# One inference step with windowed attention and PEER retrieval: attention as one sequence of 32 heads, softmax shares on ScalarE, 64 candidate key sums instead of 256

## The chip, the cores and the metric

One NeuronCore of one Trainium2 chip runs the whole program. The metric is the time of one execution on the device in microseconds (us), as a median of several. The engines are TensorE (PE, its weight loads PEld), VectorE (DVE), ScalarE (ACT), GpSimd (POOL) and SyncE (SP). Each works through its own list of instructions in order, and semaphores tie the lists together.

## The reference

Two layers, for 128 prompt tokens (one tile of 128, group P) and 512 latent tokens (four tiles, group S). Each layer computes, per token group:

```python
h = x * (1 + scale1) + shift1
q, k, v, su, sv = split(h @ w_in)              # 8 query heads, 2 kv heads of 64; su, sv of 512 go through gelu
attn = softmax([sink, q k^T / 8 + mask]) @ v   # P: its own block; S: neighbour blocks + 128 cached keys, rotary q, k
sg   = su * (w_s @ layer_norm(sv) + b_s)       # 8 groups, 128x128 position mixing
x  = layer_norm(ALPHA * x + gate1 * (concat(attn, sg) @ w_o)) * g1 + b1
h2 = x * (1 + scale2) + shift2
# PEER: per token and each of 8 heads
s1, s2 = (q half 1) @ key1.T, (q half 2) @ key2.T        # 128 scores each
t1, i1 = top_k(s1, 16);  t2, i2 = top_k(s2, 16)
top, pos = top_k(t1[:, None] + t2[None, :], 16)          # of 256 sums
idx = i1 * 128 + i2 at pos;  g = softmax(top)
y = sum over 8 x 16 experts of gelu(u_tab[idx] . h2) * g * v_tab[idx]
x  = layer_norm(ALPHA * x + gate2 * y) * g2 + b2
```

Since t1 and t2 are sorted, the sum of place i of t1 and place j of t2 (from 0) has at least (i+1)(j+1)-1 sums that are no smaller; the best 16 sums therefore lie among the pairs with (i+1)(j+1) <= 16.

The modulation vectors of both layers (24 pieces of 512 columns from w_mod, 2 MB each) are computed once, spread over the first group P of layer 0. Outputs are both x and the prompt's k and v.

## The kernel before

**Stages of a layer.** Group P runs through projection, attention, output projection, norm, PEER queries and key scores; then group S does the same with four tiles. Then come a dense PEER stage over all 128 blocks of the U table (PE, loop over b, tiles 3 and 4), the building of one-hot matrices and gates (DVE and PE), and the dense V stage (128 blocks, tiles 3, 4, 1). Tiles 0, 1 and 2 take their U rows by gather instead (POOL, line 548, 128 rows of 4 KB per partition, so 512 KB a gather, ring of 8 slots), and DVE multiplies each gathered row set with h2 and sums (`dot_rows`, line 1079); tiles 0 and 2 do the same with V rows (`add_rows`, line 1097).

**What sets the order.** There is no planner. `plan_jobs` (line 140) lists which PSUM bank each product takes and in which order; each engine's code is written out in an order that fits, and waits are counted per bank (`full`, `emptied`). SP's list holds the weight slots (ring of 8 slots of 512 KB, `w_ring`), and the row broadcasts: before the first `query` slot it waits for the last `yT` and then loads five rows into `row5`, lines 413 to 421. PE follows the same order (`attend`, line 652), ACT likewise (line 845), DVE likewise (line 1301 and the loop at line 1354).

**Attention before (per tile).** PE transposes the queries (line 649), makes three heads' scores (line 662), then the spatial gate (line 686); per head it makes one more head's scores, waits for the shares, transposes them (line 696), and weighs the values in two halves (line 672) after heads 5 and 7. DVE takes a head's scores out of PSUM with mask and maximum (line 1318) and, two heads later, adds the sink, takes the reciprocal and multiplies the exponentials (lines 1309 to 1311). ACT makes the exponentials (lines 855, 857) and copies transposed shares out of PSUM (line 863). In group S the DVE puts two `dot_rows` of tile 0 after each head. All four `norm_sv` (line 1293) come ahead of the first tile's attention, 32 of the 128 rows go into `take_qk` (line 1276), 16 come ahead of the norms and 16 between them.

**Choosing (per tile).** `half_keys` (line 1103) takes the best 16 of 128 scores, 16 times. `best_pairs` (line 1123) writes 4 heads x 256 sums and takes the best 16 of each head with five instructions over 256 columns; it runs twice. `split_positions` (line 1142) turns a place of the 256 into a pair. `pick` (line 1151) looks up the indices. ACT takes the softmax's exponential in `top_softmax` (line 883); for tile 0 it stands at the end of group P on ACT, ahead of group S's first copies at line 895. Tile 0 is chosen at the end of P, tile 1 at the end of S, tiles 3 and 4 in the dense U stage (ACT has `top_softmax(3)` after block 44), tile 2 in the dense V stage.

## Time and profile before

| | us |
|---|---|
| median of 3 runs (4259.37 to 4267.57) | 4263.49 |
| the profiled execution, its own time | 4257.01 |
| its span, first to last instruction | 4255.2 |
| PE busy, mean granted clock 0.914 | 3651.7 |
| DVE busy | 3039.6 |
| POOL busy | 1679.7 |
| ACT busy | 552.8 |
| moved by DMA | 1263.24 MB, 297 GB/s on average |

Read it so: a large busy share of PE or DVE does not say that the engine bounds a stage; which wait ends last in a stage does. "PEclk" is the clock granted to TensorE: 1.00 is 2.4 GHz, 0.50 is 1.2 GHz, and numbers between are a mix of the two within the stretch. A DMA share near 1 means that all 16 DMA engines are occupied.

### The profile page before, as it was taken

How to read it: one execution, taken by the hardware profiler on the slowest of the kernel's cores; microseconds unless marked ns; L12 is line 12 of the kernel's file. 1: busy time of each engine (PE TensorE's matmuls, PEld its weight loads, DVE VectorE, ACT ScalarE, POOL GpSimd, SP SyncE). 2: the span in 40 equal slices, each digit the busy share in tenths (PEclk: the TensorE clock that was granted, in tenths of full speed). 3: DMA queues.
4: the chain of work that ended last, by engine and by line, in shares of the span. 5: the costliest groups of instructions: out<-in, count | busy, mean ns of one | idle time of the engine just before them, and what ended most of it. 6: DMA issues, size and time to landing. Idle time of an engine off the chain costs nothing.

```text
span 4255.2 us, 38282 instructions
## 1 busy us (share of the span) xinstructions
PE 3651.7 (86%) x12502; PEld 2179.4 (51%) x12502; DVE 3039.6 (71%) x6640; ACT 552.8 (13%) x1349; POOL 1679.7 (39%) x1410
## 2 busy tenths in 40 slices
PE   8889478999997689898986846899999868989897
PEld 2334244588896434343435424458888743434333
DVE  0348865889957897656665888578996689766567
ACT  0101230111122200000001013011112220000000
POOL 3225640524312146556510465052341214555453
PEclk9899679999998999999988866999999899999998
DMA  9667762989986679999964676388998758999995
GB/s 319 234 206 300 257 218 93 341 312 349 341 318 253 242 285 381 395 397 393 395 244 160 251 268 213 117 307 300 350 370 303 273 208 319 351 393 397 397 391 233
DMA packets 458901, 1263.24 MB, mean 297 GB/s; under 512 B 40448, under 2 KB 143616, under 8 KB 452560
## 3 DMA queue, kind: packets, MB, share of 16 engines
q0 software_dynamic: 198912, 721.61, 45.3%
q1 hardware_dynamic: 234384, 455.22, 30.2%
q10 hardware_dynamic: 25408, 83.96, 4.9%
q8 instruction: 101, 1.65, 0.2%
q14 instruction: 96, 0.79, 0.1%
HBM read 1173.81 MB, written 86.84 MB: 296 GB/s over the span
## 4 chain that ended last, share of the span: by engine, by line
PE 41%; DVE 33%; DMA 19%; issue 3%; POOL 3%; ACT 1%; SPq 0%; DVEq 0%; ACTq 0%
DMA w_ring<-in_peer_v_dram 11%; PE P L811 10%; DVE ring L1079 8%; PE P L784 7%; PE P L760 6%; DMA ring<-in_peer_u_dram,eidx 5%; PE T L811 4%; DVE late L1097 3%; PE P L626 3%; DVE h L1229 3%; POOL ring L548 3%; DVE h L1225 2%; PE O L584 2%; DMA h<-acts_d 2%; PE V L584 2%
## 5 line engine op out<-in xcount | busy, mean ns | idle before, releaser
L548 POOL DMA_INDIRECT ring<-in_peer_u_dram,eidx x768 | 940.0, 1224 | 1398.8 <-DVE ring L1079 857.0
L811 PE MATMUL P<-w_ring,area 128*128 128x512 f32 x2048 | 959.8, 613 | 136.0 <-DMA w_ring<-in_peer_v_dram 74.1
L548 POOL DMA_INDIRECT ring<-in_peer_v_dram,eidx x512 | 656.4, 1282 | 916.9 <-DVE late L1097 453.4
L1079 DVE SCALAR_TENSOR_TENSOR ring<-ring,h 128x1024 f32<-128x1024 f32 x768 | 918.3, 1222 | 115.0 <-DMA ring<-in_peer_u_dram,eidx 106.1
L784 PE MATMUL P<-hT,w_ring 128*128 128x256 f32 x4096 | 900.8, 380 | 16.9 <-ACT late L954 16.7
L784 PEld LDWEIGHTS P<-hT,w_ring 128*128 128x128 f32 x4096 | 775.5, 191 | 121.6 <-ACT late L954 18.0
L811 PEld LDWEIGHTS P<-w_ring,area 128*128 128x128 f32 x2048 | 401.3, 197 | 655.3 <-issue 571.4
L811 PE MATMUL T<-w_ring,hT 128*128 128x512 f32 x1024 | 480.2, 592 | 0.0
L1097 DVE SCALAR_TENSOR_TENSOR h<-ring,dots,h 128x1024 f32<-128x1024 f32 x254 | 325.8, 1282 | 33.0 <-DMA ring<-in_peer_v_dram,eidx 17.3
L1097 DVE SCALAR_TENSOR_TENSOR late<-ring,dots,late 128x1024 f32<-128x1024 f32 x254 | 325.8, 1283 | 18.6 <-DVE late L1097 0.5
L811 PEld LDWEIGHTS T<-w_ring,hT 128*128 128x128 f32 x1024 | 194.6, 190 | 245.8 <-issue 245.8
L794 PE MATMUL T<-h 128*128 128x128 f32 x1536 | 229.2, 297 | 89.5 <-DVE h L1229 89.3
L760 PE MATMUL P<-hT,w_ring 128*128 128x128 f32 (+1 forms) x1024 | 287.3, 442 | 3.0 <-issue 2.2
L794 PEld LDWEIGHTS T<-h 128*128 128x128 f32 x1536 | 207.6, 206 | 115.0 <-issue 111.8
L1225 DVE TENSOR_TENSOR h<-qT,cst 128x512 f32<-128x512 f32 x192 | 131.7, 686 | 148.4 <-PE T L794 85.9
L760 PEld LDWEIGHTS P<-hT,w_ring 128*128 128x128 f32 x1024 | 158.4, 196 | 127.0 <-issue 122.7
L1229 DVE TENSOR_SCALAR h<-cst,qT 128x128 f32<-128x128 f32 x768 | 212.7, 339 | 0.0
L1239 DVE TENSOR_TENSOR area<-h,hT 128x256 f32<-128x256 f32 x128 | 54.3, 424 | 211.6 <-DMA h<-acts_d 175.8
L954 ACT ACTIVATE late<-P 128x256 f32<-128x256 f32 x256 | 97.9, 383 | 767.8 <-PE P L784 423.4
L696 PE MATMUL T<-ident,probs 128*128 128x128 f32 x120 | 34.9, 428 | 137.1 <-DVE probs L1311 137.1
L1239 DVE TENSOR_TENSOR area<-h,area 128x256 f32<-128x256 f32 x128 | 54.4, 425 | 123.9 <-DMA h<-acts_d 70.3
L626 PE MATMUL P<-w_ring,hT 128*128 128x512 f32 x320 | 141.5, 602 | 1.5 <-issue 1.5
(190 smaller groups left out, 2952.4 us busy)
## 6 DMA issues: line engine op xcount, KB each, us to landing
w_ring<-in_peer_uT_dram SPq DMA_DIRECT2D x256, 512.0 KB
w_ring<-in_peer_v_dram SPq DMA_DIRECT2D x256, 512.0 KB
ring<-in_w_mod_dram POOLq DMA_DIRECT2D x96, 512.0 KB, 5.9
gate_d<-area ACTq DMA_DIRECT2D x48, 1024.0 KB
w_ring<-in_peer_wq_dram SPq DMA_DIRECT2D x64, 512.0 KB
acts_d<-late ACTq DMA_DIRECT2D x128, 256.0 KB
h<-acts_d SPq DMA_DIRECT2D x64, 512.0 KB
w_ring<-in_w_in_dram SPq DMA_DIRECT2D x48, 512.0 KB
```

The source lines that it names most:

```text
L548: pool.indirect_dma_start(out=ring[:, b, :], out_offset=None, in_=tables["uv".index(phase)], in_offset=bass.IndirectOffsetOnAxis(ap=eidx[: ...
L584: mm = pe.matmul(out[0:2, :], cT[:, c, :], m_slots[:, u % MR, c % 2, :], start=c == 0, stop=c == DC - 1)
L626: mm = pe.matmul(out[:, :], hT[:, c, t * P:(t + 1) * P], w_ring[:, ws[4 * n + q], c % 2, :], start=c == 0, stop=c == DC - 1)
L760: mm = pe.matmul(out[:, 0:nt * P], w[:, c % 2, j * P:(j + 1) * P], hT[:, c, 0:nt * P], start=c == 0, stop=c == DC - 1)
L784: mm = pe.matmul(out[:, 0:TOKENS], w[:, c * P:(c + 1) * P], hT[:, c, TOKENS:2 * TOKENS], start=c == 0, stop=c == DC - 1)
L794: mm = pe.matmul(out[:, j * P:(j + 1) * P], oh_b[:, n % 2, j, :], oh_a[:, n % 2, j, :], start=True, stop=True)
L811: mm = pe.matmul(bank[ACC[2 * t + half]][:, :], w, uv_ring[:, held[b], half * 512:(half + 1) * 512], start=b == 0, stop=b == KEYS - 1)
L1079: dve.scalar_tensor_tensor(ring[:, b, :], ring[:, b, :], 1.0, h2[:, k, :], ALU.mult, ALU.mult, accum_out=dots[:, k, row:row + 1]).then_inc ...
L1097: dve.scalar_tensor_tensor(acc[k], ring[:, b, :], dots[:, k, row:row + 1], acc[k], ALU.mult, ALU.add).then_inc(row_used[b], 1)
L1225: dve.tensor_tensor(oh_b[:, n % 2], slotT[:, 1, ts].unsqueeze(2).to_broadcast([P, QUAD, KEYS]), iota128.unsqueeze(1).to_broadcast([P, QUAD ...
L1229: ins = dve.tensor_scalar(oh_a[:, n % 2, j, :], iota128, slotT[:, 0, t:t + 1], slotT[:, 2, t:t + 1], ALU.is_equal, ALU.mult)
L1239: dve.tensor_tensor(wexp_T[:, b % 4, :].rearrange("p (s t) -> p s t", t=SUB), act_in[:, b // 4 % 2, b % 4, :].rearrange("p (s t) -> p s t" ...
```

## The change

1. Group S's four tiles of eight heads run as one sequence of 32 on PE, ACT and DVE. Scores stay three heads ahead across tile borders. On PE the gate comes after head 2, the next tile's query transposes after head 4, the first half of the weighing and the transposed gate after head 6, and the second half after head 1 of the next tile.
2. The multiplication of a head's exponentials by its share moves from DVE to ACT (`den_ready`), one head behind; DVE's share of a head is taken one head late, not two.
3. `norm_sv` runs inside the sequence, after head 0 of each tile. The `dot_rows` are laid otherwise: 16 rows with the keys and values (none with the queries), 24 ahead of attention, 72 in it, and 16 behind it, ahead of the residuals.
4. ACT's `top_softmax(0)` moves behind group S's eight copies at line 895.
5. Prompt key scores go to a place of their own for all 16 half heads, so ACT waits for no free slot of `key_ring` there.
6. `best_pairs` builds 64 sums a head (1x16, 3x8, 4x4, 8x1) for all eight heads at once, four instructions, and its five instructions a head run over 64 columns. `split_positions` finds the pair with 12 instructions over all heads.
7. SP loads three of group P's five rows (gate1, ln1 gain and bias) into free parts of `area` ahead of the `w_o` slots, after a wait for the modulation rows; in S the three come where they did. The two others count on a semaphore of their own, awaited before their first use.

Fragments in this order: tiles, SP, PE, ACT (attention, `top_softmax`, prompt keys), DVE (sums, positions, attention, rows). Of attention on the three engines, `best_pairs` and `split_positions` only the new side is shown; the old side stands in the functions above.

```diff
-row5 = area[:, 0:5120].rearrange("p (r n) -> p r n", r=5)
+row5 = {g: [area[:, i * D:(i + 1) * D] for i in places]
+for g, places in (("P", (1, 3, 5, 0, 2)), ("S", (0, 1, 2, 3, 4)))}
...
+prompt_keys = area[:, 4096:6144].rearrange("p (j n) -> p j n", j=2 * PH)
...
     for kind, n, w, c0, width in plan:
+        first_rows = ((GATE1, mod_rows[l, gi, 0]), (LN1G, ln1_g[l]), (LN1B, ln1_b[l]))
+        if kind == "out" and n == 0 and g == "P":
+            for j in range(2):
+                sp.wait_ge(mod_stored[l][j], 16 * 4)
+            for r, src in first_rows:
+                sp.dma_start(row5[g][r], src.partition_broadcast(P)).then_inc(rows_in, 16)
         if kind == "query" and n == 0:
             sp.wait_ge(full[BANK["yT", g, last]], full_at(("yT", g, last), l))
-            if g == "P":
-                for j in range(2):
-                    sp.wait_ge(mod_stored[l][j], 16 * 4)
-            for r, src in ((GATE1, mod_rows[l, gi, 0]), (LN1G, ln1_g[l]), (LN1B, ln1_b[l]),
-                           (SCALE2, mod_rows[l, gi, 2]), (SHIFT2, mod_rows[l, gi, 1])):
-                sp.dma_start(row5[:, r, :], src.partition_broadcast(P)).then_inc(rows_in, 16)
+            if g == "S":
+                for r, src in first_rows:
+                    sp.dma_start(row5[g][r], src.partition_broadcast(P)).then_inc(rows_in, 16)
+            for r, src in ((SCALE2, mod_rows[l, gi, 2]), (SHIFT2, mod_rows[l, gi, 1])):
+                sp.dma_start(row5[g][r], src.partition_broadcast(P)).then_inc(late_rows_in, 16)
         for q in range(4):
...
+    nt = len(GROUPS[g])
+    heads = [(t, h) for t in range(nt) for h in range(HEADS)]
+    queries(g, 0)
+    for t, h in heads[:AHEAD]:
+        score(g, t, h)
+    for n, (t, h) in enumerate(heads):
+        if n + AHEAD < len(heads):
+            score(g, *heads[n + AHEAD])
         job = ("pT", g, t, h)
         out = begin(job)
+        pe.wait_ge(share_ready, l * (TILES * HEADS) + (GROUPS[g][t] * HEADS + h + 1))
+        for i in range(len(blocks(t)) if g == "S" else 1):
             mm = pe.transpose(out[:, i * P:(i + 1) * P], exps[h % 4][:, i * P:(i + 1) * P], ident[:])
         finish(mm, job)
+        if h == 1 and t:
+            weigh(g, t - 1, 1)
+        if h == 2:
+            gate(g, t)
+        if h == 4 and t + 1 < nt:
+            queries(g, t + 1)
         if h == 6:
+            weigh(g, t, 0)
+            gated_T(g, t)
+    weigh(g, nt - 1, 1)
...
+        if 0 < n <= len(heads):
+            t, h = heads[n - 1]
+            lo_col, hi_col = mask_cols(g, t)
+            act.wait_ge(den_ready, l * (TILES * HEADS) + (GROUPS[g][t] * HEADS + h + 1))
+            act.activation(exps[h % 4][:, 0:hi_col - lo_col], exps[h % 4][:, 0:hi_col - lo_col], ACT.Copy,
+                           scale=den[:, h:h + 1]).then_inc(share_ready, 1)
+        if n > 1:
+            t, h = heads[n - 2]
+            lo_col, hi_col = mask_cols(g, t)
+            job = ("pT", g, t, h)
+            act.activation(pT[:, h // 4, 0:(hi_col - lo_col) // P, h % 4 * P:(h % 4 + 1) * P],
+                           ready(job)[:, 0:hi_col - lo_col].rearrange("p (i n) -> p i n", n=P), ACT.Copy
                            ).then_inc(emptied[BANK[job]], 1)
+            if h == 2 and t:
+                summed_T(t - 1)
+            if h == 4 and t + 1 < nt:
+                queries(g, t + 1)
+            if h == 7:
+                job = ("yT", g, t)
+                act.activation(hT[:, 4:8, t * P:(t + 1) * P],
+                               ready(job)[:, :].rearrange("p (c n) -> p c n", c=4), ACT.Copy
+                               ).then_inc(emptied[BANK[job]], 1)
+    summed_T(nt - 1)
...
         act.activation(hT[:, c, 0:nt * P], ready(job)[:, 0:nt * P], ACT.Identity,
                        scale=mcol[:, l, 8 + c, gi:gi + 1],
                        bias=mcol[:, l, c, gi:gi + 1]).then_inc(emptied[BANK[job]], 1)
+    if g == "S":
+        top_softmax(0)
     for n, dst in ((2, su), (3, sv)):
...
                                ACT.Copy)
-            if j > 8:
-                act.wait_ge(key_used, l * (4 * PH) + (gi * 2 * PH + j - 8))
-            act.activation(key_ring[:, (j - 1) % 8, :], src[:, 0:P], ACT.Copy
-                           ).then_inc(emptied[BANK[job]], 1)
+                if j > 8:
+                    act.wait_ge(key_used, l * (2 * PH) + (j - 8))
+            act.activation(key_ring[:, (j - 1) % 8, :] if g == "S" else prompt_keys[:, j - 1, :], src[:, 0:P],
+                           ACT.Copy).then_inc(emptied[BANK[job]], 1)
             if j % 4 == 0:
                 modulation(("query", j // 4 - 1))
     modulation("end")
-    if g == "P":
-        top_softmax(0)
...
 def best_pairs(half):
+    pair = best[:].rearrange("p (h a) j -> p h a j", a=2)
+    a, b = pair[:, :, 0, :], pair[:, :, 1, :]
+    if half == 0:
+        note(dve.tensor_tensor(cand[:, :, 0:16], a[:, :, 0:1].to_broadcast([P, PH, 16]), b, ALU.add))
+        for at, i, n in ((16, 1, 3), (40, 4, 4)):
+            m = 8 if i == 1 else 4
...
+def split_positions():
+    note(dve.tensor_copy(ixf[:], best_ix[:]))
+    note(dve.tensor_single_scalar(part, pos[:], 3, ALU.logical_shift_right))
+    link(dve.tensor_single_scalar(quart, pos[:], 2, ALU.logical_shift_right))
+    link(dve.tensor_scalar(hi[:], part, 1.0, 0.0, ALU.subtract, ALU.max))
+    link(dve.scalar_tensor_tensor(hi[:], quart, -6.0, hi[:], ALU.add, ALU.max))
+    link(dve.scalar_tensor_tensor(hi[:], pos[:], -48.0, hi[:], ALU.add, ALU.max))
+    note(dve.tensor_scalar(first, hi[:], 8.0, 8.0, ALU.mult, ALU.add))
+    link(dve.tensor_scalar(lo[:], hi[:], 4.0, 24.0, ALU.mult, ALU.add))
+    link(dve.scalar_tensor_tensor(first, hi[:], 16.0, first, ALU.mult, ALU.min))
+    link(dve.tensor_tensor(first, first, lo[:], ALU.min))
+    link(dve.scalar_tensor_tensor(first, hi[:], 48.0, first, ALU.add, ALU.min))
+    link(dve.tensor_tensor(lo[:], pos[:], first, ALU.subtract))
...
+            empty(dve.tensor_tensor_reduce(exps[h % 4][:, 0:hi_col - lo_col], out[:, 0:hi_col - lo_col],
+                                           mask[:, lo_col:hi_col],
                                            HD ** -0.5, sink[:, h:h + 1], ALU.add, ALU.max,
                                            maxs[:, k % 2, h:h + 1]), job)
             dve.tensor_scalar(negmax[:, k % 2, h:h + 1], maxs[:, k % 2, h:h + 1], -1.0, None,
                               ALU.mult).then_inc(probs_max, 1)
+        if n:
+            shares(*heads[n - 1])
+        if n < len(heads):
+            if h == 0:
+                norm_sv(g, t)
+            if h == 5:
+                job = ("gate", g, t)
+                out = ready(job)
+                link(dve.tensor_tensor(tmp[:].rearrange("p (s d) -> p s d", d=HD),
+                                       out[:, :].rearrange("p (s d) -> p s d", d=HD),
+                                       bsT[:].unsqueeze(2).to_broadcast([P, SGG, HD]), ALU.add))
+                empty(dve.tensor_tensor(su[:, t, :], su[:, t, :], tmp[:], ALU.mult), job)
+            if g == "S":
+                prompt_rows(2 if h == 3 else 1)
...
+    dve.wait_ge(late_rows_in, (2 * l + (list(GROUPS).index(g) + 1)) * 32)
...
     for n in range(2):
         for t in range(nt):
             take_qk(g, n, t)
-            if latent:
+            if latent and n:
                 prompt_rows(2)
+    if latent:
+        prompt_rows(12)
     modulation("projected")
     dve.wait_ge(layer_in, (l + 1) * (16 * 8))
+    attend(g)
+    dve.wait_ge(rows_in, (2 * l + (gi + 1)) * 48)
     if latent:
         prompt_rows(8)
-    for t in range(nt):
-        norm_sv(g, t)
-        if latent:
-            prompt_rows(2)
-    for t in range(nt):
-        attend(g, t)
-    dve.wait_ge(rows_in, (2 * l + (gi + 1)) * 80)
     for t in range(nt):
         for n in range(2):
             residual(g, n, t)
...
```

## Rows read from the trace of the kernel before

**Rows 1.** Busy time by stretch: us, then PE, PEld, DVE, ACT, POOL, PEclk, DMA share, GB/s.
```profile
470.00:630.00 160.00, 104.22 (x354) 63.66 (x355) 126.25 (x330) 52.90 (x138) 87.48 (x67) 0.67 0.67 223
...
832.00:1316.00 484.00, 473.27 (x2309) 418.83 (x2308) 380.52 (x968) 77.46 (x172) 144.32 (x127) 0.99 0.89 328
...
1455.00:2188.00 733.00, 679.70 (x1536) 297.08 (x1535) 523.68 (x836) 41.52 (x128) 397.66 (x312) 0.96 0.99 371
```

**Rows 2.** Timeline where group S begins, layer 0: start us, us, instruction, [idle before <-releaser].
```profile
300.89 1.23 DVE L1126 TENSOR_TENSOR probs<-best 128x1024 f32<-128x1024 f32 x1
...
324.83 3.56 PE L721 MATMUL T<-ident,x 128*128 128x128 f32 x16 [23.77 <-ACT hT L895]
...
341.44 0.23 DVE L1176 TENSOR_SCALAR eidx<-tmp 128x128 uint32<-128x128 f32 x1
...
353.70 0.69 DVE L1267 TENSOR_TENSOR area<-T,cst 128x512 f32<-128x512 f32 x1 [12.03 <-issue]
```

**Rows 3.** Groups of DVE instructions by form, whole span: count | busy us, mean ns | idle before.
```profile
L1113 DVE MAX8 best<-left 128x8 f32<-128x128 f32 x160 | 47.1, 295 | 5.5
...
L1131 DVE MAX8 top<-probs 128x8 f32<-128x256 f32 x80 | 34.2, 428 | 2.7
```

**Rows 4.** Timeline of DVE at group S's residuals, layer 0.
```profile
640.61 0.69 DVE L1341 TENSOR_TENSOR tmp<-P,area 128x512 f32<-128x512 f32 x1 [15.33 <-DMA area<-mod_rows]
...
656.04 0.69 DVE L1341 TENSOR_TENSOR tmp<-P,area 128x512 f32<-128x512 f32 x1
...
658.63 0.69 DVE L1341 TENSOR_TENSOR tmp<-P,area 128x512 f32<-128x512 f32 x1 [1.18 <-PE P L626]
```

**Rows 5.** DVE by stretch, group S of layer 0: us, DVE busy, PEclk, DMA share, GB/s.
```profile
353.70:406.10 52.40, 51.16 (x101) 1.00 1.02 395
406.10:431.10 25.00, 19.37 (x33) 1.00 1.03 405
431.10:470.10 39.00, 36.91 (x93) 0.53 0.75 258
```

**Rows 6.** Chain of the end, pieces at layer 0: start us, us, what.
```profile
139.69 3.65 PE V L686 x16
...
446.11 4.67 DVE ring L1079 x8
```

**Rows 7.** Timeline of DVE through one head of tile 2.
```profile
528.60 0.74 DVE L1318 CUSTOM_DVE_ANT_0 probs<-P,mask,sink 128x512 f32<-128x512 f32 x1
...
529.86 0.49 DVE L1311 TENSOR_SCALAR work<-work,den 128x512 f32<-128x512 f32 x1
530.26 1.22 DVE L1079 SCALAR_TENSOR_TENSOR ring<-ring,h 128x1024 f32<-128x1024 f32 x1
...
532.55 0.74 DVE L1318 CUSTOM_DVE_ANT_0 work<-P,mask,sink 128x512 f32<-128x512 f32 x1
```

**Rows 8.** Waits from 300 to 702 us: who <- whom: us, times, longest.
```profile
DVE probs L1318 <- PE P L662: 25.1, 3, 9.5
```

**Rows 9.** Timeline of PE in the same stretch.
```profile
527.56 2.07 PE L662 MATMUL P<-kT,qT 64*128 64x384 f32 x4
530.49 1.09 PE L696 MATMUL T<-ident,work 128*128 128x128 f32 x4 [0.86 <-DVE work L1311]
...
539.27 5.40 PE L672 MATMUL O<-h,v_sb 128*128 128x512 f32 x8
```

**Rows 10.** Groups of ACT instructions by form, one tile (508 to 551 us).
```profile
L857 ACT ACTIVATE probs<-probs,negmax 128x512 f32<-128x512 f32 x4 | 2.8, 706 | 0.0
```

**Rows 11.** Timeline in the dense U stage, layer 0, ACT and PE.
```profile
1007.96 0.31 ACT L885 ACTIVATE gsm<-gsm 128x128 f32<-128x128 f32 x1 [9.46 <-DVE gsm L1139]
...
1010.02 2.50 PE L784 MATMUL P<-hT,w_ring 128*128 128x256 f32 x5 [8.91 <-ACT late L954]
```

**Rows 12.** Waits from 1525 to 1600 us, in the dense V stage.
```profile
PE P L811 <- DVE area L1239: 15.8, 4, 9.0
```

**Rows 13.** Busy time by stretch there, columns as in rows 1.
```profile
1540.00:1560.00 20.00, 9.79 (x23) 4.12 (x22) 18.86 (x54) 0.62 (x2) 2.87 (x2) 0.83 0.56 192
```

More of the change, by code:

```diff
@@ L305, in build @@
         part = left[:].bitcast(U32).rearrange("p (h j) -> p h j", h=PH)
+        first = left[:].rearrange("p (h j) -> p h j", h=PH)
         hi = sb("hi", [P, PH, TOPK])
         lo = sb("lo", [P, PH, TOPK])
+        quart = lo[:].bitcast(U32)
         r1 = sb("r1", [P, PH, TOPK])
@@ new lines, in score @@
+                def score(g, t, h):
+                    job = ("score", g, t, h)
+                    if h == 0:
+                        taken(("qT", g, t))
+                    out = begin(job)
+                    a = HD * (h // 4)
+                    for i, kb, n in runs(blocks(t) if g == "S" else [0]):
+                        mm = pe.matmul(out[:, i * P:(i + n) * P], qT[a:a + HD, h % 4, :],
+                                       kT[a:a + HD, kb:kb + n, :].rearrange("p t n -> p (t n)"), start=True, stop=True)
+                    finish(mm, job)
@@ new lines, in weigh @@
+                def weigh(g, t, kv):
+                    keyb = blocks(t) if g == "S" else [0]
+                    out = begin(("attn", g, t)) if kv == 0 else bank[BANK["attn", g, t]]
+                    taken(("pT", g, t, 4 * kv + 2))
+                    taken(("pT", g, t, 4 * kv + 3))
+                    for i, kb in enumerate(keyb):
+                        mm = pe.matmul(out[:, :], v_pad[:, kb, HD * kv:HD * kv + P], pT[:, kv, i, :],
+                                       start=kv == 0 and i == 0, stop=kv == 1 and i == len(keyb) - 1)
+                    if kv == 1:
+                        finish(mm, ("attn", g, t))
@@ L688, in attend, with gated_T @@
                     finish(mm, job)
-                    for h in range(HEADS):
-                        if h + AHEAD < HEADS:
-                            score(h + AHEAD)
+                def gated_T(g, t):
+                    taken(("gate", g, t))
+                    job = ("yT", g, t)
+                    out = begin(job)
+                    for c in range(4):
+                        mm = pe.transpose(out[:, c * P:(c + 1) * P], su[:, t, c * P:(c + 1) * P], ident[:])
+                    finish(mm, job)
@@ L692, in attend @@
+                def attend(g):
+                    nt = len(GROUPS[g])
+                    heads = [(t, h) for t in range(nt) for h in range(HEADS)]
+                    queries(g, 0)
+                    for t, h in heads[:AHEAD]:
+                        score(g, t, h)
+                    for n, (t, h) in enumerate(heads):
+                        if n + AHEAD < len(heads):
+                            score(g, *heads[n + AHEAD])
                         job = ("pT", g, t, h)
                         out = begin(job)
-                        pe.wait_ge(share_ready, l * (TILES * HEADS) + (k * HEADS + h + 1))
@@ L909, in _ @@
                     modulation("projected")
-                    for t in range(nt):
-                        attend(g, t)
+                    attend(g)
                     modulation("summed")
@@ L1011, in link, with note @@
                     dve.wait_ge(vchain, chain[0])
+                def note(ins):
+                    chain[0] += 1
+                    ins.then_inc(vchain, 1)
                 def ready(job):
@@ L1137, in softmax_in @@
+                    for h in range(4 * half, 4 * half + 4):
+                        link(dve.max(top[:, h, 0:8], cand[:, h, :]))
+                        link(dve.max_index(pos[:, h, 0:8], top[:, h, 0:8], cand[:, h, :]))
+                        link(dve.match_replace(cand[:, h, :], top[:, h, 0:8], cand[:, h, :], LOWEST))
+                        link(dve.max(top[:, h, 8:16], cand[:, h, :]))
+                        link(dve.max_index(pos[:, h, 8:16], top[:, h, 8:16], cand[:, h, :]))
                 def softmax_in(k):
@@ L1299, in norm_sv, with attend, shares @@
                     dve.wait_ge(sv_ready, l * TILES + (GROUPS[g][t] + 1))
-                def attend(g, t):
-                    k = GROUPS[g][t]
-                    lo_col, hi_col = mask_cols(g, t)
-                    width = hi_col - lo_col
-                    def shares(h):
+                def attend(g):
+                    nt = len(GROUPS[g])
+                    heads = [(t, h) for t in range(nt) for h in range(HEADS)]
+                    def shares(t, h):
+                        k = GROUPS[g][t]
                         n = l * (TILES * HEADS) + (k * HEADS + h + 1)
```

179 lines of the change are left out of this document (54 added, 125 removed).

## The prediction, made before the changed kernel was run

> **What bounds the kernel now.** I read the chain of the end first: it runs through the stages one after another, so each stage has to be read for its own limit. Busy time by stretch gives three kinds [rows 1]. The dense V stage (1455 to 2188 us) has all DMA engines occupied (0.99). The dense U stage (832 to 1316) is PE's: 473 of 484 us. In the attention of group S (470 to 630) no engine is full: DVE 126 of 160, PE 104 of 160 at a granted clock of 0.67, DMA 0.67. So attention is bound by how DVE and PE wait for each other. Then the timeline where group S begins [rows 2]: PE stands idle for 23.8 us, because ACT, which must copy its first transposes, sits in `top_softmax(0)` and waits for DVE's choosing of tile 0; DVE finishes choosing at 341.7 and waits in its turn 12.0 us for PE's first product, until 353.7. Layer 1 repeats every pattern below, so each number counts twice unless I say otherwise.
>
> **Choosing gets shorter.** One sorting instruction costs 428 ns over 256 columns and 295 over 128 [rows 3], 1.04 ns a column, so about 0.23 us over 64: 0.20 less, 40 instructions a tile, -8.0 us. The sums: two instructions of 1.23 us [rows 2] become four with 128, 192, 128 and 64 elements; from the 0.23 us of the 128-element instruction [rows 2] and the slope above I estimate 1.2 together (bounds 0.9 and 2.5), -1.3. `split_positions`: ten small instructions on half the heads become twelve on all; at 0.23 to 0.3 each that is 3.2 plus gaps against some 2.3, +1.2. Net -8.1 a tile: 40.8 us (300.9 to 341.7) become 32.7, to 333.6.
>
> **Group S begins earlier.** With `top_softmax(0)` behind the copies, PE transposes and makes the query products (before: from 324.8, first result taken at 353.7) while DVE chooses: they need 29 us from 300, so they are there before 333.6. DVE then starts at 333.6 rather than 353.7: -20.1. If PE were not early, only the 8.1 would be left; if PE's own start were free too, still DVE sets this.
>
> **From there to the end of attention DVE is the bound; the sum of its work.** Before it took 353.7 to 625.3 (the 640.6 of the first residual less its wait of 15.3 [rows 4]) = 271.6. After, part by part:
> - taking queries, keys, values: 52.4 us with 32 gathered rows in them [rows 5]; in the chain four rows (eight records) take 4.67 [rows 6], and their last 0.08 is covered, so 1.15 a row; 16 rows fewer, 34.0.
> - 24 rows at once: before, 16 rows took 25.0 us with DMA at 1.03 [rows 5], 1.56 each; the gathers bound this: 37.5 (bounds: 27.6 at DVE's pace; 43 if the two weight streams overlap it worse, by a tenth more than 1.56).
> - attention: a head takes 528.60 to 532.55 = 3.95 with two rows; the multiplication takes 0.40 of it (529.86 to 530.26) [rows 7]; 3.55 x 32 = 114. Four norms: 39.0 less 16 rows [rows 5] is 20.6. Four gates of two 0.69 us instructions (like the first of [rows 4]), 5.6. Eight extra rows, 9.2. Together 149.
>
> That is 220.5. The three tile borders, at which DVE waited 25.1 us for PE's scores [rows 8], are gone as far as PE keeps up. PE per head: 2.07 for scores and 1.09 for transposes [rows 9], 3.16 of 3.55 at 1.2 GHz, and per tile 16 records of weighing (8 took 5.40 at a clock that rose in them [rows 9], so 3.4 to 6.9 a half), a gate of 3.65 at 1.2 GHz [rows 6] and two small transposes. At 1.2 GHz that is 25 + 13.7 + 3.7 + 2.2 = 45 against DVE's 37 a tile; at 2.4 GHz about 24. PE has three heads' scores in hand, and the long DVE piece after head 0 (5.2 us of norm) falls where PE catches up. I take 2 us of waits in all; bounds 0 and 4 x 8 = 32. The Trainium skill ("TensorE: Matmul & The Clock Gate", section on what is actually happening) says that the default clock is the throttled one and sustained activity releases it. The row agrees: the 5.4 us of eight records against 6.9 shows it rising while PE works without a pause; by that rule a PE that falls behind runs at 2.4 GHz until it has caught up, and the waits are near 0.
>
> ACT gains the multiplication: the exponential over the same columns is 0.71 us [rows 10], and I take the same for the multiplication and for the copy out of PSUM, so ACT needs about 0.3 + 0.9 (with its sum) + 0.7 + 0.7 = 2.6 of 3.55 a head. Nothing waits for it but PE, which has slack. Result: 222.5 instead of 271.6, -49 (bounds -25 and -61).
>
> **Behind attention something is given back.** DVE now waits for three broadcast rows and only then takes 16 gathered rows. Before, five rows and 15.3 us; SP sends them after the last transposed gate, which now comes about 2.5 us later behind DVE's last head (estimated from half a tile's weighing ahead of it, 3.4 or more [rows 9]); three of five rows land 4 to 5 earlier: wait about 12. Then 16 x 1.15 = 18.4. First residual 30 us after attention instead of 15.3. PE first makes two tiles of products and then needs the first tile's h2; before, it had 2.6 us to spare (h2 at 656.0, the second product at 658.6 [rows 4]), and the products now start 2.5 later, so 15 - 5 = +10 on the path. DVE's 12.5 us a tile (15.4 from 640.6 to 656.0, less the 2.9 it waited in them) stays under PE's: DVE waited for PE at the next tile too, 1.2 us [rows 4]. Bounds +4 (rows land at once) and +15.
>
> Group S per layer: -20 - 49 + 10 = -59; both layers -118. Layer 1's stretch before is 4 us longer than layer 0's by the same reading, so -122.
>
> **Group P.** Its three early rows: in layer 0 SP now waits for the modulation rows before it loads `w_o`; the slots still come before PE wants them, cost 0 (bounds 0 and +4). The residuals of P wait for PE's second product anyway, so early rows win nothing. The gate (3.65 [rows 6]) moves from under the norm into the chain of heads, the norm behind head 0: I take +1.5 a layer (bounds -3 and +5), +3. The prompt keys' own place: 0; DVE's scanning limits there and ACT's wait stood beside it (bounds -3 and 0).
>
> **Dense U stage.** ACT waits 9.5 us for DVE's choice of tile 3, and PE 8.9 us for ACT [rows 11]. DVE reaches it 8.1 (tile 1's choosing) + 9.3 (sums and sorting of tile 3) = 17 earlier, so the wait goes. PE was also at the low clock after it: -10.7, in layer 1 about -9. Later two small PE waits under tile 4's `best_pairs` go, -1.5 each. What is late next is PE itself. Both layers -23 (bounds -8 and -26: the gathered rows under full DMA could hold DVE back).
>
> **Dense V stage.** DMA-bound as a whole, but around tile 2's `best_pairs` PE waits 15.8 us for DVE [rows 12] while the DMA share falls to 0.56 [rows 13]: there DVE is the bound, and its 8.1 come off: both layers -16 (bounds 0, if the full DMA later takes it back, and -19).
>
> **Sum.** -122 + 3 - 23 - 16 = -158. From the profiled execution: 4257.0 - 158 = 4099. The median of the runs shown is 6.5 above that execution: 4105.5, forecast 4105.
>
> **The rivals.**
> - *PE bounds attention at 1.2 GHz.* For it: clock 0.67 in the stretch, and 45 us of PE work a tile against 37. Against it: the clock rises in unbroken work [rows 9]. Eight waits of 8 us: 4105 + 60 = 4165. Chance 0.08.
> - *The gains in the dense stages are swallowed by the DMA*, which is at 0.99 and 0.89 [rows 1]. Against it: the share falls to 0.56 where DVE holds PE. 39 us less gain: 4144. Chance 0.10.
> - *The order stays but PE starts group S no sooner* (weights or banks missing): 12 us a layer, 4129. The weights of the first two products were loaded before 300. Chance 0.04.
> - *Slower: ACT in lock step.* ACT's list is exponential, multiplication, copy of the transposed shares; the copy waits for PE, PE's transposes for the multiplication, DVE's next sum for the exponential. If PE falls so far behind that ACT stands in the copy each time, a head costs the whole ring: scores 2.1, maximum 0.9, exponential 1.2, sum 0.3, multiplication 0.7, transposes 1.1, copy 0.7, rows 2.3 = 9.3 instead of 3.55. 32 x 5.7 x 2 = +365: 4470. It decides above 2.5 us more a head (158/64), a head of 6.0. Against it: DVE has a head's exponential behind it when it needs the sum, and three scores ahead. The Trainium skill says ScalarE's queue is strict FIFO ("TensorE: Matmul & The Clock Gate", what it says of queue depths); no row here shows ACT passing a waiting instruction, and by that rule this rival needs only one late PE product per head. Chance 0.03.
>
> **How the numbers follow.** The forecast's case has 0.75, its own range 4078 to 4130 from the bounds of its terms, not all at one end. The range for 8 in 10 goes to the PE rival on the upper side and to the low ends of attention and P on the other: 4065 to 4168. A difference under 0.2% (8.5 us) can't be told from none here. Faster 0.95, same 0.02, slower 0.03.
>
> **What would show it.** In the changed profile: DVE's first group S instruction right behind the choosing, no wait of some 12 us; no wait of 7 to 10 us of DVE on PE's scores in attention; a head at 3.5 us; a wait for broadcast rows of about 12 and PE idle some 8 us ahead of the first transposes of h2; no wait of ACT for `top_softmax(3)`; half the 15.8 in the dense V stage. Wrong if heads take over 4 us, if PE's clock in attention stays near 0.5 with DVE waiting for scores, or if the dense stages are as long as before.

## The result, and the profile after

The changed kernel takes 4103.6 us (median of 4, 4093.0 to 4109.8) where the kernel before took 4264.8 in the same runs: a ratio of 0.9621, 95% interval 0.9595 to 0.9647. The forecast was 4105. The profiled execution went from 4257.0 to 4098.2, that is -158.8, against a sum of -158. Two executions far above the others of their kernel are left out of the medians below: 4163.3 us in run 10 (granted clock 0.899, the others 0.933) and 10735.4 us in run 5. Terms in us, by stretch of the two traces:

| step | forecast | layer 0 | layer 1 |
|---|---|---|---|
| choosing a tile | -8.1 | -8.7 | -8.7 |
| group S's first DVE instruction, from the start of choosing | -20.1 | -20.7 | -20.9 |
| from there to the last head | -49 | -53.6 | -59.8 |
| last head to group S's first query product | +10 | +16.8 | +17.7 |
| group S, first transposes to first query product | -122 both | -57.5 | -63.0 |
| group P, its first transposes to group S's | +3 both | -1.7 | +2.9 |
| dense U | -23 both | -12.1 | -12.5 |
| dense V | -16 both | -10.7 | -4.0 |

The last head ends here with DVE's last work on its share. Dense U is taken from PE's first to its last product there (before: 831.7 to 1316.5 us), dense V from DVE's first to its last multiplication by the expert weights there (before: 718.0 us in layer 0, 717.4 in layer 1).

Busy time by stretch of the kernel after, columns as in rows 1, which these answer to: attention, dense U, dense V.

```profile
412.00:550.00 138.00, 102.22 (x354) 63.11 (x355) 133.50 (x356) 64.75 (x164) 97.06 (x71) 0.70 0.79 273
...
772.00:1245.00 473.00, 471.94 (x2316) 418.53 (x2315) 355.88 (x982) 77.73 (x173) 146.22 (x128) 1.00 0.91 336
1385.00:2108.00 723.00, 675.42 (x1536) 296.12 (x1536) 515.41 (x841) 41.50 (x128) 397.00 (x312) 0.97 1.00 377
```

In attention DVE is busy 133.5 of 138 us, where before it had 126 of 160 [rows 1]: now it is the bound. PE's granted clock is 0.70, not better than 0.67, and DVE waits for no score all the same. Dense U is full of PE work (471.9 of 473).

The start of group S, layer 0, from the timelines of PE and of DVE (as rows 2):

```profile
298.74 1.09 PE L741 MATMUL T<-ident,x 128*128 128x128 f32 x8
300.76 1.32 PE L741 MATMUL T<-ident,x 128*128 128x128 f32 x8 [0.93 <-ACT hT L927]
```
```profile
331.50 0.23 DVE L1226 TENSOR_SCALAR eidx<-tmp 128x128 uint32<-128x128 f32 x1
331.76 0.69 DVE L1316 TENSOR_TENSOR area<-T,cst 128x512 f32<-128x512 f32 x1
...
345.43 0.29 DVE L1316 TENSOR_TENSOR k_sb<-P,cst 128x128 f32<-128x128 f32 x1 [4.23 <-PE P L619]
```

PE waits 0.93 us for ACT where it waited 23.8 [rows 2], and DVE goes from its last choosing instruction to the first query product without a wait. What is late next is the keys' product, 4.2 us. The sorting instruction, grouped by form over the whole span (as rows 3):

```profile
L1175 DVE MAX8 top<-probs 128x8 f32<-128x64 f32 x80 | 18.2, 228 | 2.5
```

One head of tile 1 in DVE's timeline (as rows 7): from one scores instruction to the next it takes 3.42 us, with the same two gathered rows.

```profile
463.04 0.74 DVE L1369 CUSTOM_DVE_ANT_0 probs<-P,mask,sink 128x512 f32<-128x512 f32 x1
...
464.10 0.16 DVE L1360 RECIPROCAL den<-den 128x1 f32<-128x1 f32 x1
464.18 1.20 DVE L1115 SCALAR_TENSOR_TENSOR ring<-ring,h 128x1024 f32<-128x1024 f32 x1
...
466.46 0.75 DVE L1369 CUSTOM_DVE_ANT_0 probs<-P,mask,sink 128x512 f32<-128x512 f32 x1
```

Behind attention, DVE and then PE (as rows 4):

```profile
562.90 1.22 DVE L1115 SCALAR_TENSOR_TENSOR ring<-ring,h 128x1024 f32<-128x1024 f32 x1 [13.15 <-DMA area<-in_ln_b_dram]
...
579.35 1.22 DVE L1115 SCALAR_TENSOR_TENSOR ring<-ring,h 128x1024 f32<-128x1024 f32 x1 [1.83 <-DMA ring<-in_peer_u_dram,eidx]
...
585.02 0.68 DVE L1396 TENSOR_TENSOR tmp<-P,area 128x512 f32<-128x512 f32 x1
```
```profile
558.53 27.63 PE L636 MATMUL P<-w_ring,hT 128*128 128x512 f32 x64
597.49 1.97 PE L651 MATMUL T<-ident,h 128*128 128x128 f32 x8 [11.33 <-DVE h L1407]
599.25 15.29 PE L636 MATMUL P<-w_ring,hT 128*128 128x512 f32 x32
...
640.29 1.97 PE L651 MATMUL T<-ident,h 128*128 128x128 f32 x8 [10.26 <-DVE h L1407]
```

DVE waits 13.2 us for broadcast rows and takes 16 gathered rows until 585.0; PE stands 11.3 us before the first h2 (14.0 in layer 1), and its next 32 products take 15.3 us, not 13.9. The last two waits that the forecast named, in dense U (772 to 1245) and dense V (1470 to 1530), who waits for whom as in rows 8 and 12:

```profile
PE P L803 <- ACT late L985: 1.1, 1, 1.1
```
```profile
PE P L830 <- DVE area L1288: 8.5, 3, 4.8
```

PE's stall of 8.9 us [rows 11] is gone, and 8.5 of 15.8 us [rows 12] are left.

### The profile page after: what moved, and what is told of

It reads as the page before. It is cut to its first block, busy times and chain, and to the rows that moved or that the text cites. A ratio compares the mean times of both kernels' runs of the same rounds, so it can differ in the third digit from the quotient of the medians.

```text
span 4096.4 us, 38314 instructions
## 1 busy us (share of the span) xinstructions
PE 3631.4 (89%) x12502; PEld 2169.6 (53%) x12502; DVE 2917.0 (71%) x6600; ACT 586.6 (14%) x1429; POOL 1693.4 (41%) x1410
## 4 chain that ended last, share of the span: by engine, by line
PE 49%; DVE 23%; DMA 22%; POOL 2%; issue 2%; ACT 1%; SPq 0%; DVEq 0%; ACTq 0%
PE P L803 17%; DMA w_ring<-in_peer_v_dram 13%; PE P L830 9%; PE P L779 7%; DVE ring L1115 5%; DMA acts_d<-late 5%; PE T L830 4%; DVE h L1278 3%; DVE late L1133 3%; POOL ring L558 2%; PE P L636 2%; PE O L594 2%; PE T L813 2%; DVE h L1274 2%; PE V L594 2%
## 5 line engine op out<-in xcount | busy, mean ns | idle before, releaser
L558 POOL DMA_INDIRECT ring<-in_peer_u_dram,eidx x768 | 955.0, 1244 | 1298.6 <-DVE ring L1115 783.5
L813 PE MATMUL T<-h 128*128 128x128 f32 x1536 | 229.7, 298 | 85.4 <-DVE h L1278 85.4
L1005 ACT ACTIVATE area<-T 128x512 f32<-128x512 f32 x192 | 114.6, 597 | 197.2 <-PE T L813 196.8
## 6 DMA issues: line engine op xcount, KB each, us to landing
w_ring<-in_peer_v_dram SPq DMA_DIRECT2D x256, 512.0 KB, 16.4
```

Source lines behind the costliest of these rows:

```text
L558: pool.indirect_dma_start(out=ring[:, b, :], out_offset=None, in_=tables["uv".index(phase)], in_offset=bass.IndirectOffsetOnAxis(ap=eidx[: ...
L813: mm = pe.matmul(out[:, j * P:(j + 1) * P], oh_b[:, n % 2, j, :], oh_a[:, n % 2, j, :], start=True, stop=True)
L1005: act.activation(gate_st[:, s % 2, :, col * QUAD:(col + 1) * QUAD], ready(job)[:, :].rearrange("p (t e) -> p e t", t=QUAD), ACT.Copy).then ...
```

## The experiments

Each kernel is the changed one with the edit shown; stretches are from the profiled execution of each against that of the changed kernel. "S to last head" runs from group S's first transposes to the last head's share: 250.8 and 254.2 us in the changed kernel. "Behind it" runs from there to the first query product: 93.4 and 94.7. Both take the start of DVE's last reciprocal as the last head's share, so they lie 0.2 us off the table's stretches.

**1. The softmax of tile 0 back at the end of group P.**

```diff
-                    if g == "S":
-                        top_softmax(0)
...
                     modulation("end")
+                    if g == "P":
+                        top_softmax(0)
```

> The changed kernel with one step undone: ACT's top_softmax(0) stands again at the end of group P. The changed kernel took 4103.6 us. Theory A (the start of group S is worth what the forecast said beyond the shorter choosing, and the projection on PE passes a late start on to the first head): ACT is free at about 315, PE begins group S there and not at 298.7, DVE's first product comes at about 345 and not at 331.8 in layer 0, and the first head moves from 407.1 by 13 to 17 us; over two layers +25 to +34, total 4129 to 4138. Theory B (the 24 gathered rows ahead of attention are held by the gathers, which took 37.1 us where DVE alone would need 28, and so take a late start back): +4 to +8 a layer, total 4112 to 4120.

Measured: 4131.7 us, +28.1; S to last head +15.0 and +17.5. Timeline at group S's start:

```profile
314.60 0.31 ACT L917 ACTIVATE gsm<-gsm 128x128 f32<-128x128 f32 x1 [62.36 <-DVE gsm L1183]
315.63 5.48 PE L741 MATMUL T<-ident,x 128*128 128x128 f32 x24 [14.19 <-ACT hT L927]
...
344.69 0.69 DVE L1316 TENSOR_TENSOR area<-T,cst 128x512 f32<-128x512 f32 x1 [11.36 <-PE T L619]
```

Theory A holds: PE is held for 14.2 us by ACT, and the delay reaches the first head whole. The gathers take nothing back: in this run the 24 gathered rows end at 423.8 us, and PE's own first scores start at 422.0, where in the changed kernel the two stand at 407.0 and 406.1. The order on ACT alone is thus worth 28 us of the 161, more than the 12 a layer of the forecast's split.

**2. Sums of 256 again.**

```diff
-        cand = probs[:, 0, :].rearrange("p (h n) -> p h n", h=PH)
+        cand = probs[:].rearrange("p a (h n) -> p (a h) n", n=256)
...
-                        split_positions()
+                        split_positions(0)
+                        split_positions(1)
```

(with `best_pairs` and `split_positions` as before the change)

> The changed kernel with part 6 undone: 4 heads x 256 sums, twice, five instructions a head over 256 columns, positions split as before. Theory A (every tile's 8.7 us counts where DVE is what the next stage waits for): group S's start +8.7 a layer, dense U +12 a layer (the ACT wait for top_softmax(3) and PE's stall are back), dense V +9 in layer 0 and +4 in layer 1; together +54, total 4158. Theory B (at the start of group S the choosing now lies beside PE's first products: DVE waits 4.2 us for PE's keys product behind the queries, and the gathers behind that): start of S +0 to +4.5 a layer, the dense stages as in A; +37 to +46, total 4141 to 4150. Either way a stall of PE of some 9 us behind u block 44 must show in the dense U stage.

Measured: 4152.8 us, +49.2; S to last head +6.0 and +7.4, dense U +13.9 and +13.3, dense V +7.7 and -0.4. PE's wait in dense U is back:

```profile
PE P L803 <- ACT late L985: 9.6, 1, 9.6
```

Between the two theories: of the 8.7 us at group S's start 6.0 and 7.4 reach the last head. In layer 0 the 4.2 us wait for the keys' product is gone, and DVE's waits for gathered rows ahead of attention grew from 7.4 to 8.6 us. The shorter sums are worth 49 us, over half of it in dense U.

**3. The share's multiplication back on DVE.**

```diff
-                        dve.reciprocal(den[:, h:h + 1], den[:, h:h + 1]).then_inc(den_ready, 1)
+                        link(dve.reciprocal(den[:, h:h + 1], den[:, h:h + 1]))
+                        dve.tensor_scalar(exps[h % 4][:, 0:hi_col - lo_col], exps[h % 4][:, 0:hi_col - lo_col],
+                                          den[:, h:h + 1], None, ALU.mult).then_inc(share_ready, 1)
```

(ACT's multiplication taken out)

> The changed kernel with the multiplication by the share back on DVE (0.40 to 0.44 us a head) and away from ACT. Theory A (DVE's own work is what bounds the sequence of 32 heads: busy 33.9 of 35 us): 32 x 0.40 = +12.8 a layer, +26 in all, total 4129. Theory B (PE bounds it, at a granted clock of 0.50 to 0.79 and 23 to 28 us busy of 35, or the ring from scores to shares does): the place of the multiplication changes nothing, 0 to +5, total 4104 to 4109.

Measured: 4123.7 us, +20.1; S to last head +16.5 and +16.3. Theory A in kind: DVE's sum binds. By stretch it is 0.51 us a head, not 0.40. DVE's timeline shows the rest:

```profile
462.97 0.16 DVE L1355 RECIPROCAL den<-den 128x1 f32<-128x1 f32 x1
463.17 0.49 DVE L1356 TENSOR_SCALAR work<-work,den 128x512 f32<-128x512 f32 x1
463.57 1.22 DVE L1109 SCALAR_TENSOR_TENSOR ring<-ring,h 128x1024 f32<-128x1024 f32 x1
```

The multiplication waits for the end of the reciprocal and starts 0.20 us behind its start, and the gathered row comes 0.40 later. In the changed kernel the gathered row needs nothing of the reciprocal and starts 0.08 behind its start (464.10 to 464.18 above). So 0.60 against 0.08, that is 0.52 a head; the forecast priced the 0.40 alone [rows 7]. The median moves less than two stretches of 16.4; this profile's layer-1 dense V was 6.5 us shorter (more on that below).

**4. The 16 rows ahead of the wait for the broadcast rows.**

```diff
-                    dve.wait_ge(rows_in, (2 * l + (gi + 1)) * 48)
                     if latent:
                         prompt_rows(8)
+                    dve.wait_ge(rows_in, (2 * l + (gi + 1)) * 48)
```

> The changed kernel with DVE's wait for the three broadcast rows put behind the 16 gathered rows that follow attention, not ahead of them; nothing else changes. Theory A (the two follow one another on DVE and this alone makes PE wait 11.3 us ahead of the first transposes of h2): the 13.2 us wait is covered, the first residual stands 22 us behind attention and not 35, PE's wait is gone, and it stays at its high clock (the 32 products behind took 15.3, not 13.9 us, and the transposes 1.97, not 1.04): -13.6 a layer, -27 in all, total 4076. Theory B (rows and gathers then share the DMA and slow each other, so the broadcast rows come later than the 16 gathered rows end): no more than half, -6 a layer, total 4091.

Measured: 4076.0 us, -27.6, but by stretch less: behind the last head 85.9 and 83.8, that is -7.5 and -10.9. DVE's and PE's timelines:

```profile
566.90 1.26 DVE L1115 SCALAR_TENSOR_TENSOR ring<-ring,h 128x1024 f32<-128x1024 f32 x1 [4.83 <-DMA ring<-in_peer_u_dram,eidx]
...
578.80 0.69 DVE L1396 TENSOR_TENSOR tmp<-P,area 128x512 f32<-128x512 f32 x1
```
```profile
591.27 1.97 PE L651 MATMUL T<-ident,h 128*128 128x128 f32 x8 [3.52 <-DVE h L1407]
```

The median says A, the trace something between: the wait is covered, but the 16 rows now take 27.4 us (551.4 to 578.8) beside the broadcasts, not 22.1, and PE still waits 3.5. The 18.4 us of the two stretches are what I take as shown (the two profiled executions differ by 18.7); the other 9 of the medians lie within their spread (4093.0 to 4109.8 for the changed kernel). PE's wait was DVE's: that stands either way.

**5. Those rows split around the norms.**

```diff
                     if latent:
-                        prompt_rows(8)
+                        prompt_rows(4)
                     dve.wait_ge(rows_in, (2 * l + (gi + 1)) * 48)
...
                         norm_modulate(g, t)
+                        if latent and t < 3:
+                            prompt_rows((2, 1, 1)[t])
```

> The changed kernel, but of the 16 gathered rows behind attention 8 come ahead of DVE's wait for the broadcast rows and 8 behind the norms of tiles 0, 1 and 2 (4, 2 and 2), where DVE waits for PE's products. Against the kernel with all 16 ahead of the wait (4076.0 us), where PE still waits 3.5 and 3.8 us for h2 of tile 0. Theory A (DVE has room there: 12.5 us of its own a tile against 14.7 of PE's products): PE's wait for tile 0's h2 is gone, its clock stays up, -6 a layer, total 4064; the only long wait of PE left is that for the last tile's h2, 10.3 us. Theory B (the gathers come no faster than one in 1.3 us and now hold the norms, or the last norm moves): no gain, 4076 or more.

Measured: 4084.4 us, 8.4 above run 4 (ratios to before 0.9584 +- 0.0019 and 0.9553 +- 0.0016). Behind the last head 82.4 and 82.0: -3.5 and -1.8 against run 4, not -6. So the stretches that the edit touches are shorter, while the two dense V stages took 7.6 us more in this profile than in run 4's, which the edit doesn't touch; the totals don't decide between the two kernels. PE's timeline:

```profile
586.12 1.04 PE L651 MATMUL T<-ident,h 128*128 128x128 f32 x8
...
630.22 1.97 PE L651 MATMUL T<-ident,h 128*128 128x128 f32 x8 [13.65 <-DVE h L1407]
```

The wait for tile 0's h2 is gone as in A, and 3.4 us come back at the last tile, as in B: the rows between the norms pushed the chain of norms.

**6. Sixteen more rows out of attention, behind the last norm.**

```diff
-                                prompt_rows(2 if h == 3 else 1)
+                                prompt_rows(1 if h else 0)
...
                     if latent:
+                        prompt_rows(8)
                         expert_weights(0)
```

(on top of run 5's edit)

> As the run with the rows split, and 16 more of the 72 gathered rows taken out of attention (none at head 0, one step at every other head) and put behind the last norm, where DVE waits 24 us for the first key scores. Theory A (DVE's sum bounds the sequence of heads): 16 x 1.17 = 18.6 us a layer less, total 4064 - 37 = 4027. Theory B (PE is close behind: 26 to 28 of 35 us busy a tile at a granted clock of 0.74 to 0.79, and it becomes the bound): -5 a layer, 4054; DVE's waits for scores show it. Theory C: the late rows hold ACT's gelu and with it the first query copies, and nothing is won, 4064 or more; then the first key scores come later than 32 us behind the last norm.

Measured: 4043.9 us, -40.5 against run 5; S to last head -17.9 and -18.6 against the changed kernel. Waits of DVE from 414 to 533:

```profile
DVE work L1369 <- PE P L670: 0.4, 1, 0.4
```

Theory A: with 56 rows DVE still waits for almost no score, so PE is not yet the bound; and the late rows fall into DVE's idle time.

**7. Prompt rows and prompt keys as before.**

```diff
-                        if kind == "out" and n == 0 and g == "P":
...
+                            if g == "P":
+                                for j in range(2):
+                                    sp.wait_ge(mod_stored[l][j], 16 * 4)
...
-                        half_keys(j, prompt_keys[:, j, :], None)
+                    half_keys(j, key_ring[:, j % 8, :], l * (4 * PH) + (gi * 2 * PH + j + 1))
```

> The changed kernel with parts 5 and 7 undone (prompt key scores through the ring of eight again, all five rows of group P loaded at its first query slot). The two act in different stretches, so the trace tells them apart. Theory A, the forecast's: both are worth nothing, 4104. Theory B: the early rows are worth up to 2.7 us in layer 0, where the products of the output projection took 14.0 us after and 16.7 before (DVE, waiting for its rows, held PE's second half), nothing in layer 1; the keys nothing: 4106.

Measured: 4098.3 us, within the spread; group P's first transposes to its first query product 142.6 and 85.4 us (changed kernel 142.6 and 85.6), the output products 14.0 us in both. Theory A. What made the products 16.7 us before, in layer 0, is PE's clock. The 32 products before, and then in the changed kernel:

```profile
158.51 16.70 PE L626 MATMUL P<-w_ring,hT 128*128 128x512 f32 x32 [0.73 <-issue]
```
```profile
160.10 13.97 PE L636 MATMUL P<-w_ring,hT 128*128 128x512 f32 x32 [0.73 <-issue]
```

From 160 to 164 us the granted clock was 0.50 before and 1.00 in the changed kernel (1.00 in this run too). These 2.7 us are not of the parts undone here; why the clock rose earlier stays open.

**8. Scores two heads ahead.**

```diff
-AHEAD = 3
+AHEAD = 2
...
-            if h == 4 and t + 1 < nt:
+            if h == 5 and t + 1 < nt:
```

(the second edit on PE, ACT and in the plan of banks)

> The changed kernel with PE's scores two heads ahead and not three (the next tile's queries one head later, as their buffer demands). Theory A (in the sequence PE is never more than one head late, DVE binds at 4.4 us a head against 3.2): +0 to +4, 4104 to 4108. Theory B (the lead covers the pieces in which PE makes no scores, 3 to 5 us of weighing and 4 to 5 us of waiting for ACT's query copy, so that a shorter lead turns them into waits of DVE on scores): 2 to 5 us at two places a tile, +16 to +40 a layer, 4136 to 4184.

Measured: 4115.6 us, +12.0; S to last head +6.8 and +6.7. Waits of DVE from 415 to 560:

```profile
DVE probs L1369 <- PE P L670: 6.1, 4, 2.2
```

Neither size was right; the kind is B's, since waits on scores appear. A lead of three hides all of PE's pieces without scores, a lead of two all but 6 us a layer.

**9. Group P's norm first.**

```diff
-                            if h == 0:
+                            if h == 0 and g == "S":
                                 norm_sv(g, t)
...
+                    if g == "P":
+                        norm_sv(g, 0)
```

> The changed kernel with group P's norm_sv ahead of its first head on DVE, as before the change, and not behind head 0; group S keeps its order. In the trace of the changed kernel group P's part from its first transposes to its queries is 2.9 us longer in layer 1 than before. Theory A (the norm of 5.2 us behind head 0 holds that head's share and so all of the eight, and this is the 2.9): -2 to -3 a layer, total 4098 to 4100. Theory B (the gate of PE, which now stands between the heads, is what costs it): nothing, 4104. The trace decides, since the time can hardly: shares of layer 1 begin 38 us or 41 us behind the layer's first transposes.

Measured: 4096.6 us, within the spread; group P's first transposes to its first query product in layer 1 85.6 to 83.2 us (-2.4), its shares beginning 38.4 and not 40.9 us in; layer 0 -0.9. Theory A: by the table's own stretch, which runs on to group S's first transposes, the norm's place is 2.0 of the +2.9.

**10. The 16 rows inside attention.**

```diff
                     if latent:
-                        prompt_rows(8)
...
-                                prompt_rows(2 if h == 3 else 1)
+                                prompt_rows(2 if h in (1, 3, 6) else 1)
```

> The changed kernel with the 16 gathered rows behind attention moved into it (11 steps a tile and not 9), so that DVE only waits for the broadcast rows there, as before the change. Theory A (DVE's sum is the bound of the sequence; behind attention the 16 rows cost what PE waits for them): +18.7 us a layer in attention, and behind it first residual some 14 us after the last head, PE's wait of 11.3 and 14.0 gone with 2.3 of its clock: +5 in layer 0, +3 in layer 1, total 4112. Theory B (PE or ACT is the bound of the sequence and DVE has room): attention no longer, -13 a layer, total 4077.

Measured: 4107.3 us, +3.8; S to last head +18.9 and +17.4, behind it 78.9 and 78.7. Theory A: a row costs 1.1 to 1.2 us in attention, DVE's own time for it, and the 16 rows cost 14.5 and 16.0 behind it. Moving them was worth 1 to 4 us a layer and no more.

**11. All of it together.** Run 6 with 12 rows ahead of the wait, two behind each of the first three norms, 14 behind the last, and run 9's edit.

```diff
+                        prompt_rows(6)
                     dve.wait_ge(rows_in, (2 * l + (gi + 1)) * 48)
...
+                        if latent and t < 3:
+                            prompt_rows(1)
                     if latent:
+                        prompt_rows(7)
                         expert_weights(0)
```

> The run with the rows split and late (4043.9 us), with 12 rows and not 8 ahead of the wait for the broadcast rows, two behind the norms of tiles 0, 1 and 2, 14 behind the last, and group P's norm first. In that run PE waited 13.7 us for the last tile's h2, and 10.3 in the changed kernel; DVE waited 6.4 us for rows and 4.7 for PE ahead of the first norm. Theory A (the four rows behind tile 0's norm had pushed the chain of norms back, and there is room for four more rows ahead of it): PE's last wait is 10.3 again, -3.4 a layer, and group P -2.5 a layer, total 4032. Theory B (twelve rows ahead of the wait take as long beside the broadcasts as the 16 did, 27.5 us, and hold the first h2): -5 from group P at most, +3 a layer, 4045.

Measured: 4035.2 us (5 runs, 4034.7 to 4042.8), ratio to before 0.9473 (0.9455 to 0.9492): 68 us below the changed kernel, 8.7 below run 6. Behind the last head 81.1 and 80.8. PE waits for the last h2:

```profile
609.15 1.97 PE L651 MATMUL T<-ident,h 128*128 128x128 f32 x8 [11.57 <-DVE h L1409]
```

13.7 became 11.6 (12.7 in layer 1), not 10.3: A, with two thirds or less of its size. This is the fastest kernel of the study.

## Why the prediction was right

**Choosing.** 228 ns over 64 columns against the 0.23 us taken from a straight line through two widths [rows 3]. As run 2 shows, the shorter choosing counts at group S's start, in dense U and in layer 0's dense V, 49 us in all, and not measurably in layer 1's dense V (-0.4).

**Group S's start.** The reading that an engine (ACT) waiting at the end of one stage held the first transposes of the next was right; run 1 puts the wait back and gets its price. The reason why it pays was incomplete: I priced DVE's start only. PE's projection, whose first product now starts at 306.1 us and not at 331.0, bounds the first head as well (PE's first scores at 406.1, DVE's first head at 407.1), so both engines had to come forward.

**Attention.** DVE's sum was the bound (runs 3, 6 and 10 all move by DVE's own work). In its parts: queries, keys and values with 16 rows 38.1 us (34.0 forecast, the difference is the 4.2 us wait for keys), 24 rows 37.1 (37.5), the sequence 142.6 (151). The last is too high because I priced all heads as four-block heads at 3.55: they are 3.42 (the wait on the reciprocal went too, run 3), and 3.29 with three blocks, and the 2 us of waits didn't come. Layer 1's sum fell from 275.4 to 215.6, 6.2 more than layer 0's; I have not taken that apart. The lower bound of 25 doesn't follow from its own terms: 32 us of waits would still leave 19. The rival in which PE at 1.2 GHz bounds attention had its condition met in part and still did not happen. By stretch, columns as in rows 1:

```profile
412.00:447.00 35.00, 23.37 (x69) 16.39 (x70) 33.89 (x94) 14.52 (x40) 24.58 (x18) 0.50 0.88 310
...
482.00:517.00 35.00, 28.25 (x104) 17.14 (x104) 33.98 (x89) 17.97 (x43) 25.26 (x18) 0.79 0.78 264
```

At the start, mostly heads with three blocks, PE ran at 1.2 GHz all the time and was busy 23.4 of 35 us; where the heads have four blocks it was busy 28.3 of 35, at a granted clock of 0.79. The 45 us of PE work a tile, all at 1.2 GHz, thus never came. With a lead of two heads, 6.1 us of waits appear (run 8). On the other rival, ACT in lock step: the Trainium skill ("TensorE: Matmul & The Clock Gate", on queue depths) calls ScalarE's queue strict FIFO, and no row here contradicts it, but ACT is busy 64.8 of 138 us, and DVE waited for it in no head of the sequence.

**Behind attention.** The mis-sized term: +10 forecast, +16.8 and +17.7 measured, outside its bounds of 4 to 15. The wait was nearly right (13.2 for 12). Two things were missed. Sixteen rows took 22.1 us, not 18.4: while DVE waits, only eight can lie in the ring, and the last four of the sixteen came in 7.6 us. And PE, having stood 11.3 us, did the next 8 transposes in 1.97 and not 1.04 us and the 32 products in 15.3 and not 13.9, so 2.3 us more. That price of a stall beyond the stall was in no term of the sum. Together 1.2 + 3.7 + 2.3 = 7.2 us, about the 6.8 that were missing in layer 0. The too small give-back (34.5 us in both layers for 20) and the too small gain in attention (113.4 for 98) cancel, and that group S came out at -120.5 of -122 is luck to that extent: with only one of the two misses the total would have been some 15 us off.

**Group P.** +1.3 of +3; run 9 shows the norm behind head 0 as the cause of 2.0 of layer 1's +2.9, run 7 that early rows and own keys are worth nothing. Layer 0's -1.7 holds the 2.7 us by which the output products became shorter at the higher clock; no term of the forecast had them, so the closeness here is luck too.

**Dense U and V.** -24.6 of -23 and -14.7 of -16. In U the stall behind u block 44 went, and only PE was late next. In V the DMA took part of it back in layer 1: PE's waits on weight slots sum to 46 us there, before to 38, and in layer 0 to 38, before to 36. The layer-1 stage took 705.6 to 713.5 us, on DVE as in the table, in the changed kernel and the eleven experiments, mostly kernels that change nothing there; what makes these 8 us stays open, and it is the reason why effects below 10 us are read from stretches here and not from medians.

## What to carry to other kernels

Look at the end of each stage for an engine that waits for something it needs only later: moved past the next stage's first work it cost nothing, and it was worth 28 us. When filler work (here gathered rows) must be spread, put it where its engine waits for something else: the kernel with the same 128 rows a layer took 68 us less (some 3 of them from group P) when 12 lay under the broadcast wait, 6 behind the first three norms and 14 under the wait for the first key scores, instead of 16 in attention, where DVE's sum was the bound, and 16 behind a wait that covered none of them.

## What the runs showed that I had not expected

Broadcast rows and gathered rows slow each other: 16 gathered rows take 22.1 us behind the broadcasts and 27.4 beside them (run 4), with the DVE instruction itself at about 1.22 us in both. From issue to landing, from 549 to 590 us, a gather took 5.8 us in the median in the changed kernel and 11.3 in run 4, and the broadcast of the norm's bias, the last of the three that DVE waits for, 7.1 and 11.9. And taking an instruction that advanced a DVE sequence by 0.40 us out of it saved 0.51 us a head, because the wait on the reciprocal ahead of it went as well.
